# A two-block transformer on one Trainium2 core: the first feed-forward linear in two passes by tokens, one of them among the last gathers of the expert rows

## The reference

```python
# end of the first block, for each token (8 heads x 16 picks = 128 experts of 16,384)
a = einsum('cd,ced->ce', xb, u_tab[eb])          # dot with each gathered u row
w = gb * gelu(a)
out = einsum('ce,ced->cd', w, v_tab[eb])         # weighted sum of the gathered v rows
h = h + out
# start of each of the two layers of the second block (D_FF = 2816)
x = x + 0.5 * swiglu(rms_norm_2(x, ffn1_norm[l]), ffn1_w13[l], ffn1_w2[l])
def swiglu(h, w13, w2):
    a, g = split(h @ w13, 2)
    return (silu(a) * g) @ w2
```

## Time and profile before

| | before |
|---|---|
| device time, median of 3 runs | 4279.62 us (4277.93 to 4279.63) |
| span of the profiled execution | 4274.8 us |
| time outside its span | not given for that execution; the runs' median stands 4.8 us above the span |
| PE busy | 3978.5 us, 93% of the span |
| gathers' DMA (q0) | 536.90 MB, 29.8% of 16 DMA engines |
| weights' and other loads (q1) | 258.86 MB, 19.2% |
| end of the last matmul of the up projection, layer 0 | 1980 us |

### The profile page before, as it was taken

The page is one execution under the profiler, slowest core; times in us unless marked ns, Lnnn a source line. Parts: engine busy times, 40 slices in busy tenths (PEclk is TensorE's granted clock), DMA queues, the critical chain, the costliest instruction groups (busy, mean ns, idle before and its releaser), DMA issues.

```text
span 4274.8 us, 50156 instructions
## 1 busy us (share of the span) xinstructions
PE 3978.5 (93%) x15936; PEld 2775.4 (65%) x15936; DVE 2155.4 (50%) x4180; ACT 1299.2 (30%) x2803; POOL 2261.2 (53%) x2978
## 2 busy tenths in 40 slices
PE   9999987878887777999999999999999999999998
PEld 7877633333333333688867767888888867768887
DVE  8376877767767765432155544331332165534322
ACT  3142332222222222432233433322332134323322
POOL 7646543333333333566655546666665745536664
PEclk9999999899999999999999999999999999999999
DMA  5242899999999999333312212323233312213332
GB/s 148 87 107 77 342 427 427 427 427 427 427 427 427 421 427 427 124 98 93 100 65 72 67 57 91 102 93 100 95 98 96 97 52 70 82 46 107 97 95 83
DMA packets 181079, 805.06 MB, mean 188 GB/s; under 512 B 40656, under 2 KB 43392, under 8 KB 115328
## 3 DMA queue, kind: packets, MB, share of 16 engines
q0 software_dynamic: 73728, 536.90, 29.8%
q1 hardware_dynamic: 82112, 258.86, 19.2%
q10 hardware_dynamic: 25024, 6.69, 0.8%
HBM read 796.87 MB, written 4.59 MB: 187 GB/s over the span
## 4 chain that ended last, share of the span: by engine, by line
PE 70%; DMA 17%; DVE 8%; ACT 2%; issue 1%; DVEq 1%; ACTq 0%; SPq 0%; POOLq 0%; POOL 0%
PE bank L815 19%; PE bank L817 18%; PE bank L816 18%; DMA rows_o<-in_peer_uv,of_picks_int 7%; PE bank L1213 5%; DMA rows_x<-in_peer_uv,of_picks_int 4%; DMA rows_w<-in_peer_uv,of_picks_int 3%; DMA work<-in_peer_uv,of_picks_int 3%; DVE rows_o L2510 1%; PE bank L909 1%; DVE rows_w L2510 1%; DVE rows_x L2510 1%; PE bank L1273 1%; PE bank L1405 1%; PE bank L1393 1%
## 5 line engine op out<-in xcount | busy, mean ns | idle before, releaser
L674 POOL TENSOR_TENSOR wl<-raw,wh 128x256 fp32r<-128x256 f32 (+1 forms) x1928 | 1518.7, 819 | 640.5 <-ACT wh L1822 604.7
L815 PE MATMUL bank<-xh,wh 128*128 128x512 f32 x2304 | 916.2, 398 | 0.0
L817 PE MATMUL bank<-xh,wl 128*128 128x512 f32 x2304 | 898.2, 390 | 0.0
L816 PE MATMUL bank<-xl,wh 128*128 128x512 f32 x2304 | 897.2, 389 | 0.0
L1822 ACT ACTIVATE wh<-raw 128x1024 fp32r<-128x1024 f32 x296 | 312.1, 1056 | 687.9 <-PE bank L817 558.7
L815 PEld LDWEIGHTS bank<-xh,wh 128*128 128x128 f32 x2304 | 432.5, 188 | 128.2 <-issue 34.3
L817 PEld LDWEIGHTS bank<-xh,wl 128*128 128x128 f32 x2304 | 432.4, 188 | 92.3
L816 PEld LDWEIGHTS bank<-xl,wh 128*128 128x128 f32 x2304 | 433.0, 188 | 87.4 <-issue 2.4
L2558 DVE TENSOR_TENSOR work<-bank,rstd 128x512 f32<-128x512 f32 x176 | 121.4, 692 | 537.5 <-PE bank L817 536.0
L1213 PE MATMUL bank<-rows_o,diag 128*128 128x512 f32 x592 | 294.7, 645 | 75.8 <-ACT diag L1783 75.8
L1213 PE MATMUL bank<-rows_x,diag 128*128 128x512 f32 x576 | 286.6, 645 | 65.2 <-ACT diag L1783 65.2
(11 more groups left out here) (514 smaller groups left out, 6212.3 us busy)
## 6 DMA issues: line engine op xcount, KB each, us to landing
raw<-in_w_l SPq DMA_DIRECT2D x316, 512.0 KB, 3.3
raw<-in_w_l SPq DMA_DIRECT2D x64, 448.0 KB, 3.3
raw<-in_w SPq DMA_DIRECT2D x54, 512.0 KB, 3.3
raw<-in_w_l SPq DMA_DIRECT2D x56, 256.0 KB, 2.6
raw<-in_w SPq DMA_DIRECT2D x20, 256.0 KB, 2.6
raw<-in_uq_l SPq DMA_DIRECT2D x8, 384.0 KB, 3.0
rows_o<-in_peer_uv,of_picks_int POOLq DMA_INDIRECT x148, 21.7
rows_w<-in_peer_uv,of_picks_int POOLq DMA_INDIRECT x144, 21.7
```

Source lines behind the costliest of these rows:

```text
L674: last = gp.tensor_tensor(wl[:, slot, c], raw[:, rslot, c], f32(wh[:, slot, c]), ALU.subtract)
L815: pe.matmul(bank[b][:], wh[:, slot, c], ah, start=k == 0, stop=False)
L816: pe.matmul(bank[b][:], wh[:, slot, c], al, start=False, stop=False)
L817: mm = pe.matmul(bank[b][:], wl[:, slot, c], ah, start=False, stop=k == last)
```

## The change

The up projection of layer 0 is done in two passes. The first takes tokens 0 to 255, whose x is final once the first two token blocks have been added, and stands among picks 376 to 503; the second takes tokens 256 to 511 at the old place. Each pass loads and splits all 44 weight tiles.

- The 44 tiles of the first pass are numbered ahead of layer 0 (`QUERY_END + t`). PE does 8 or 9 of their 352 blocks after each of 128 picks (`fore_step`), three matmuls of 256 columns each (`fore_up`). ACT rounds the tiles (`fore_rounded`) and POOL makes their low halves, in two parts after two fetches. DVE and ACT gate the results, with a tanh in place of the silu, into `h_fore`.
- From pick 304 the rows `x0`, `x1` and `work` are no longer used (11 buffers), from pick 350 `w0` to `w3` and `more` neither and `late` is back (7 buffers), from pick 448 `temps` is added (8).
- From pick 352 (q = 11) ACT works one pick at a time.
- In the second pass every matmul, readout, gate and split has 256 columns. Rounding is ACT's and the low halves POOL's, as before. `down1` of layer 0 reads both halves from `h_fore` in one matmul of 2 x 256 columns.
- The loop over the two layers is written out on all engines.

```diff
+QUERY_END = TILES_1
+TILES_1 += 2 * FF
...
+FORE = T // 2
+FORE_FROM, FORE_PICKS = 376, 128
+X_ROWS_TO, W_ROWS_TO = 304, 350
...
+def fore_step(n):
+
+    return min(max(n - FORE_FROM, 0), FORE_PICKS) * (2 * FF * KD) // FORE_PICKS
...
+def fore_end(j):
+
+    return FORE_FROM - 1 - (-(KD * (j + 1) * FORE_PICKS) // (2 * FF * KD))
...
+def fore_slot_free(n, lag):
+
+    return [t for t in range(2 * FF) if (fore_end(t - RING) if t >= RING else W_ROWS_TO + 6 + 2 * t) + lag == n]
...
+        row_temps = at("row_temps", [P, 2 * D], F32, region + 45056)
+        kept_end = at("kept_end", [P, D], F32, late)
+        fore_h = at("fore_h", [P, KD, FORE], F32R, base + 4 * KD * T)
+        fore_l = at("fore_l", [P, KD, FORE], F32R, base + 4 * KD * T + 4 * KD * FORE)
+        fore_work = at("fore_work", [P, 8, FORE], F32, base + 4 * KD * T * 3 + 4 * RAWS * KD * P + 8 * RING * KD * P)
...
+        LAST_ROWS = ["o0", "o1", "o2", "o3", "x2", "x3", "late"]
+        TEMPS_FROM = 14 * WINDOW
+        row_of = list(FIRST_ROWS)
+        for rows, end in ((RING_ROWS, X_ROWS_TO), (MIDDLE_ROWS, W_ROWS_TO), (LAST_ROWS, TEMPS_FROM), (LAST_ROWS + ["temps"], NB * PICKS)):
+            oldest = sorted(rows, key=lambda r: max([m for m, s in enumerate(row_of) if s == r], default=-1))
+            row_of += [oldest[m % len(rows)] for m in range(end - len(row_of))]
         row_use = [row_of[:n + 1].count(r) for n, r in enumerate(row_of)]
         row_last = [max([m for m in range(n) if row_of[m] == r], default=None) for n, r in enumerate(row_of)]
         RAW_FREE = 1 + row_of.index("raw")
...
@@ -603,10 +655,14 @@
             for s in ("br_a", "out", "query"):
                 stage1(s, "w8_1")
 
-            sp.wait_ge(p_mixed, RAW_FREE)
...
@@ -752,10 +811,18 @@
             query_low(7)
             for n in range(8, NB * PICKS):
                 fetch(n)
-
-
-            gp.wait_ge(p_mixed, ROWS_W_FREE)
-            with gp.Fori(0, DEPTH) as l:
+                for half in range(2):
+                    for t in fore_slot_free(n, 10 + half):
+                        tile = QUERY_END + t
+                        if half == 0:
+
+                            gp.wait_ge(w_hi.sem, t + 1)
+                            low_half(tile % RING, tile % RAWS, KD * P // 2)
+                        else:
+                            low_half(tile % RING, tile % RAWS, KD * P, KD * P // 2).then_inc(w_split.sem, 1)
+
...
+            def fore_sums():
+
+                pe.wait_ge(score_read.sem, score_read.at(pairs + 20, None))
+                pe.wait_ge(fore_square, KD)
+                for k in range(KD):
+                    mm = pe.matmul(score[1][:, 0:FORE], ones[:], fore_work[:, k, :], start=k == 0, stop=k == KD - 1)
+                mm.then_inc(fore_sum, 1)
+
+            def fore_up(m):
+
+                j, k = divmod(m, KD)
+                tile = QUERY_END + j
+                slot, out = tile % RING, score[j % 2][:, 0:FORE]
+                if k == 0:
+                    pe.wait_ge(w_split.sem, w_split.at(tile + 1, None))
+                    if j == 1:
+                        pe.wait_ge(fore_root, 1)
+                    elif j > 1:
+                        pe.wait_ge(fore_read, j - 1)
+                if j == 0:
+                    pe.wait_ge(fore_low, k + 1)
+                c = slice(k * P, (k + 1) * P)
+                pe.matmul(out, wh[:, slot, c], fore_h[:, k, :], start=k == 0, stop=False)
+                pe.matmul(out, wh[:, slot, c], fore_l[:, k, :], start=False, stop=False)
+                mm = pe.matmul(out, wl[:, slot, c], fore_h[:, k, :], start=False, stop=k == KD - 1)
+                if k == KD - 1:
+                    mm.then_inc(product.sem, 1)
+
             for n in range(EARLY):
                 mix(n)
             pe.wait_ge(*read_at(query, 6, None))
...
                     mix(n)
+                    if n == FORE_FROM:
+                        fore_sums()
+                    for m in range(fore_step(n), fore_step(n + 1)):
+                        fore_up(m)
             turn_back(NB - 1)
 
...
                     ready = normed_ready()
                     at_ = AT_L[up]
-                    first_two(at_, l, ready)
-                    sum_squares(l)
+                    fore = l == 0 and up == "up1"
...
                     ready = operand_ready(FF)
                     for j in range(8):
-                        linear(at_, j, l, pair(hh, hl), ready)
+                        linear(at_, j, l, (lambda k: (h_fore[:, :, 0, k, :], h_fore[:, :, 1, k, :])) if fore else pair(hh, hl), ready)
...
                     return
                 act.wait_ge(p_mixed_half, 1)
-                act.activation(kept[:, 0:T], summing[:, 0:T], ACT.Copy).then_inc(p_kept, 1)
+                act.activation(kept_end[:, 0:T], summing[:, 0:T], ACT.Copy).then_inc(p_kept, 1)
                 act.wait_ge(p_mixed, NB * PICKS)
-                act.activation(kept[:, T:2 * T], summing[:, T:2 * T], ACT.Copy).then_inc(p_kept, 1)
+                act.activation(kept_end[:, T:2 * T], summing[:, T:2 * T], ACT.Copy).then_inc(p_kept, 1)
...
+            def fore_operand(k):
+
+                if k == 0:
+                    act.wait_ge(p_added, 2)
+                    act.wait_ge(p_mixed, X_ROWS_FREE)
+                act.activation(fore_h[:, k, :], x[:, k, 0:FORE], ACT.Copy, scale=next_gain[:, k:k + 1]).then_inc(fore_high, 1)
+                act.activation(fore_work[:, k, :], x[:, k, 0:FORE], ACT.Square).then_inc(fore_square, 1)
+
+            def fore_rounded(t):
+
+                tile = QUERY_END + t
+                if t == 0:
+                    act.wait_ge(p_mixed, ROWS_W_FREE)
+                elif t >= RING:
+                    act.wait_ge(product.sem, product.at(tile + 1 - RING, None))
+                act.wait_ge(w_loaded[tile % RAWS], 16 * (tile // RAWS + 1))
+                act.activation(wh[:, tile % RING, :], raw[:, tile % RAWS, :], ACT.Copy).then_inc(w_hi.sem, 1)
+
+            def fore_norm():
+
+                act.wait_ge(fore_sum, 1)
+                inverse_root(fore_rstd, score[1][:, 0:FORE], D).then_inc(fore_root, 1)
+                act.activation(small[:, 7:8], eps[:], ACT.Gelu)
+
+            def fore_beside(n):
+
+                if n == FORE_FROM + 1:
+                    fore_norm()
+                for t in fore_slot_free(n, 2):
+                    fore_rounded(t)
+                for j in fore_at(n, 5):
+                    p = j // 2
+                    if j % 2 == 0:
+                        act.wait_ge(fore_read, j + 1)
+                        act.activation(fore_work[:, 2 + p % 2, :], fore_work[:, p % 2, :], ACT.Tanh, scale=0.5).then_inc(fore_tanh, 1)
+                    else:
+                        act.wait_ge(fore_mult, p + 1)
+                        act.activation(h_fore[:, 0, 0, p, :], fore_work[:, 4 + p % 2, :], ACT.Copy).then_inc(fore_hi, 1)
 
             act.activation(warm[:], eps[:], ACT.Sqrt)
...
                     sizes = [1] * (2 * QUAD) + [QUAD] * (WINDOW // QUAD - 2)
-                elif q == WINDOWS - 1:
-                    sizes = [QUAD] * (WINDOW // QUAD - 3) + [1] * (3 * QUAD)
+                elif q >= 11:
+                    sizes = [1] * WINDOW
...
                         act.activation(diag[:, n % DIAGS, :], ident[:], ACT.Copy, scale=weight[:, n:n + 1]).then_inc(p_diag, 1)
+                    if q >= 11:
+                        fore_beside(n0)
+                    elif q == 10:
+                        fore_operand(g)
...
                 c = PEER_OUT + k
-                high_and_square(k, None, next_gain[:, k:k + 1], (acc_read[c % 4].sem, c // 4 + 1))
-            act.wait_ge(p_pick, WINDOWS + 2)
+                high_and_square(k, None, next_gain[:, k:k + 1], (acc_read[c % 4].sem, c // 4 + 1), tokens=slice(FORE, T))
+            act.wait_ge(p_mixed, NB * PICKS)
             for t, name in consts_l:
                 act.dma_start(t[:], d[name]).then_inc(late_loaded, 16)
...
+            def fore_low_half(k):
+
+                dve.wait_ge(fore_high, k + 1)
+                dve.scalar_tensor_tensor(fore_l[:, k, :], x[:, k, 0:FORE], next_gain[:, k:k + 1], f32(fore_h[:, k, :]),
+                                         ALU.mult, ALU.subtract).then_inc(fore_low, 1)
+
+            def fore_gated(j):
+
+                p = j // 2
+                a_, t_, h_ = (fore_work[:, 2 * m + p % 2, :] for m in range(3))
+                dve.wait_ge(product.sem, product.at(QUERY_END + j + 1, None))
+                if j == 0:
+                    dve.wait_ge(fore_root, 1)
+                if j % 2 == 0:
+                    dve.tensor_tensor(a_, score[0][:, 0:FORE], fore_rstd, ALU.mult).then_inc(fore_read, 1)
+                    if p > 0:
+                        fore_rest(p - 1)
+                    return
+                dve.tensor_tensor(h_, score[1][:, 0:FORE], fore_rstd, ALU.mult).then_inc(fore_read, 1)
+                dve.wait_ge(fore_tanh, p + 1)
```

(25 more changed lines are left out.)

## The result

The changed kernel takes 4308.05 us (median of 4 runs, 4299.66 to 4310.73), against 4279.62 (4277.93 to 4280.13) before: ratio 1.0066, 95% interval 1.0054 to 1.0079. It is slower, by 28 us. The forecast was 4274, with a range up to 4306.

A forecast was written before the change was run, and what follows sets the result against it. DMA was taken to bound the gathers and PE the up projection: -72 given back, +54 bytes, +12 stalls make -6 us, so 4279.6 becomes 4274 us, with a range of 4257 to 4306.

The forecast's parts named there:

- Stalls: Gather stage with the first pass: seven buffers' turns mostly fit the DMA pace; waits cost 12 us in all.
- 4 for loads and roundings that come late later on: First pass, after its start: late weight loads and roundings cost 4 us, with some 9 us planned for a load.
- bytes: Gather stage: the first pass's 44 loads, 23.07 MB at 427 GB/s, add 54 us that nothing hides.
- I charge 3 us for that: Picks 350 to 376: DVE's expert stretches do not fit comfortably in a buffer's turn of 17.2 us; 3 us.
- The rival on buffers: Gather stage: expert stretches, low halves, roundings and late loads overrun seven buffers' turn; about 4303 us, chance 0.20.
- PE's margin: First pass: PE needs 2.72 us a pick, leaving 0.16 to recover what it loses in each stretch.
- the 3.05: First pass: picks taking more than 3.05 us, or less than 2.8, would show the prediction wrong.
- 256 columns: PE's fp32r matmuls of half width: each takes 119 ns, against 226 for 512 columns.
- The rival of the weight load: PE's matmuls: weight loads space them 188 ns apart, slowing both passes; about 4340 us, chance 0.05.
- the second pass: Up projection, tokens 256 to 511: load, rounding and low half pace it at 3.85 us a tile; 72 us given back.
- The clock: Up projection's later pass: PE keeps full clock, with gaps of 1 us a tile; a fall would show the prediction wrong.
- the rival's 50 us: Up projection's later pass: PE falls to 1.2 GHz, 5.12 us a tile, taking back 50 us; 4324 us, chance 0.04.

The follow-up runs named there:

- a2_low_earlier: Changed kernel with both parts of each first-pass low half made after one fetch, one and two picks earlier on POOL: 4283.8 us, ratio 1.0017.
- a3_no_stretch: Changed kernel without DVE's choice of experts from q = 11, copying earlier experts and gates instead: 4289.2 us, ratio 1.0022.
- a1_rows_only: Kernel before with only the changed row buffers and ACT's single picks, no first pass: 4289.14 us, ratio 1.0024.
- c3_less_pe: Changed kernel without one of the three matmuls of each first-pass block: 4309.17 us, ratio 1.0069.
- c2_half_low: Changed kernel with POOL making only columns 0 to 511 of each low half in the second pass's loop: 4273.96 us, ratio 0.9991.
- the two shared kernels: The four edits, plus DVE making one or two of the four pieces of each second-pass low half: 4269.65 and 4264.18 us.
- four edits: Changed kernel with low halves earlier, eighth buffer from pick 456, tanh and high half before rounding, tiles 2 and 3 planned later: 4278.47 us, ratio 1.0.
- d1: The four edits, plus DVE making one of the four pieces of each low half in the second pass: 4269.65 us, ratio 0.9984.

## Why the prediction was wrong, step by step

- **What fell.** The step "Stalls", and in it the term "4 for loads and roundings that come late later on, as the plan gives a load some 9 us". The stalls were put at 12 us and measured 46 (100 for the stage, less 54 for the bytes). A load among gathers took 7.2 us to its last packet (4.6 to 8.8) and 8 to 9 us from issue to ACT's start, and the plan did give about that. (The 7.8 that the prediction took from the earlier trace rows is the shorter of the two loads there; the other took 10.7, so the row already had one that the plan's 9 us do not cover.) But a plan with no slack at its shortest edge is not late once, it is late in each turn: ACT waited 106.3 us for 30 loads. I charged it as an accident of a few us. Giving the load one or two picks more took 25 of the 34 missing us back (a2_low_earlier, pick 510 at 1802.8).
- **Also too small: the stretches.** "I charge 3 us for that" was for DVE's work on the experts. Leaving it out brought 16 us by pick 510 beside the loop (a3_no_stretch), and without a first pass the buffers, stretches and all, cost 12.7 (a1_rows_only). That a stretch costs much only where the loop has used up the room of the queue fits both, and is not shown further. These 16 us and the 25 overlap and must not be added.
- **What was left out.** That the fetch into `temps` waits for the experts' choice. The stretch itself stood in the prediction, as something the queue of buffers must cover; that one fetch depends on its end, with all fetches queued behind, did not. Its price is 5.8 to 8.7 us alone (medians, dots) and 2.4 to 2.8 with the loop gone.
- **The rival on buffers.** "Seven buffers are too few" gave 4303 and was nearest to the result, but the number came out near for another reason: the buffers alone cost 11 us, and with seven buffers kept, a change of order took back 24. Its sentence on how POOL's low half, ACT's rounding and a late load meet in one turn names the right parts. It took the shared length of a buffer's turn for the cause, where what moved the time was the order that issues the load. That more buffers would have done as much is not excluded. Its other half, PE's margin, was worth nothing (c3_less_pe).
- **Right: bytes.** q1 moved 23.07 MB more (281.93 against 258.86), 54 us at 427 GB/s. Where nothing else disturbs, a pick takes 2.87 us (2.88 predicted). Over all of the first pass (376 to 504) it took 3.16, above the 3.05 that the prediction named as a sign of being wrong.
- **Right: 256 columns.** PE's rows of the changed kernel, start and length:

```profile
1661.01 0.28 PE L1314 MATMUL bank<-fore_h,wl 128*128 128x256 f32 x1
1661.13 0.28 PE L1312 MATMUL bank<-fore_h,wh 128*128 128x256 f32 x1
1661.25 0.28 PE L1313 MATMUL bank<-fore_l,wh 128*128 128x256 f32 x1
```

They start 0.12 us apart, 119 ns predicted. Each record's 0.28 us overlaps the next. The rival of the weight load is out.
- **Mis-sized: the second pass.** 3.94 us for a tile instead of 3.85, and 67 us back instead of 72. The mechanism, the chain of a weight slot, is confirmed by c2_half_low and the two shared kernels. 3.94 is also what the bytes of the earlier trace rows gave, which the prediction had as its upper value.
- **The clock.** It did fall in the second pass, which the prediction named as a sign of being wrong. The windows of the changed kernel show where:

```profile
1902.00:1922.00 20.00, 14.90 (x120) 14.21 (x118) 7.96 (x14) 8.40 (x10) 15.32 (x21) 1.00 0.39 131
1922.00:1926.00 4.00, 4.00 (x21) 4.00 (x22) 0.19 (x1) 0.51 (x1) 2.67 (x4) 0.59 0.53 141
1926.00:1946.00 20.00, 16.04 (x128) 15.34 (x127) 7.57 (x14) 9.52 (x11) 15.47 (x21) 1.00 0.40 129
1946.00:1950.00 4.00, 4.00 (x23) 4.00 (x23) 0.99 (x2) 0.72 (x1) 2.54 (x4) 0.58 0.46 143
```

Most of these 4 us ran at 1.2 GHz, the 20 us between them at 2.4 GHz, and so it goes on to 1998. Ahead of the falls PE's longest gaps, one for every two tiles, were 1.4 to 1.9 us, well above the 0.5 of single picks that the prediction compared with, and below the 2.7 between groups of four picks in the kernel before. With the gaps of c2_half_low, mostly 0.2 to 0.4 us, the clock stayed at 1.00. But the falls cost next to nothing. PE's wait for POOL was 1.91 us at 1921.97, ahead of the fall, and 0.24 at 1929.71, behind it: the slower matmuls only fill the wait. By the starts of POOL's low halves two tiles took 8.02 and 7.82 us at full clock from 1903 to 1919, and 7.92 and 7.90 over the fall. The Trainium skill (TensorE: Matmul & The Clock Gate, "HAM oscillation") tells of a loop that waits longer than it works and starts every round at the half clock; this loop works longer than it waits, and the trace shows the half clock at some rounds only. The prediction kept full clock and was wrong in that, yet rightly charged nothing, and of the rival's 50 us nothing is to be seen.
- **The sum.** -67 + 54 + 46 = +33 on the span, where 32.6 was measured. It comes out by construction, since the 46 is what the bytes leave of the stage's 100. With four edits that touch only the plan, the stage comes out at +69.7 and the time at 4278.5. So the forecast described a kernel whose plan has slack, and the one measured has none.

Still open: some 16 us of stalls remain with the four edits. Picks 350 to 390 take 114.5 us there against 97.9 before, and only some 7 of the 16.6 are bytes (3.1 MB of weights in the trace). The rest lies where the rings are reduced and the first loads and tokens' halves are made. In a1_rows_only, with the same rings and no first pass, these picks take 101.6 us, so 4 of the remaining 9 go with the rings; which of the others it is was not tried alone.

## What to carry to other kernels

A load that is issued at one engine's place in a fixed order and awaited at another's needs slack in that order above its latency amid the traffic that is there. Here, without it, the wait came back in 30 of 44 turns, and spread to what stood behind either engine. So write down the plan's shortest edge (here from the low half of tile t to the rounding of tile t + 2) and hold it against the measured latency before counting bytes. Where a chain of engines paces a stage, as in the second pass, shorten its longest link, if need be by handing a part to an engine with room.

## What was unexpected of the hardware

- Loads of one eighth the size were not eight times quicker amid the gathers: the last packet came 4.6 us after the issue, against 7.2 us at full size (medians), and ACT still waited 2.5 us each for 26 of them, against 3.5 us each for 30.
- A DVE subtraction of 256 columns with both inputs in SBUF took 670 ns where POOL's took 828, and while DVE had two of four pieces, POOL's pieces took 46 ns more than the 782 of the changed kernel. With one piece on DVE (d1) they took 870. Why fewer pieces on DVE went with slower ones on POOL was not tried.
- The clock fell to 1.2 GHz for short stretches in a loop in which PE never stood still for more than 2.0 us at a time (from 1860 to 1990), and the time of the loop did not show it, since PE was waiting for POOL anyway.
